# Gate/up biases added in PSUM by TensorE, down weights loaded in 8 KB runs: a 32-expert MoE block on one core

## What is computed

```python
def expert_block(args):
    xblk, e = args
    gu = xblk @ w_gu[e] + b_gu[e]
    x_glu = jnp.minimum(gu[:, :F], SWIGLU_LIMIT)
    x_lin = jnp.clip(gu[:, F:], -SWIGLU_LIMIT, SWIGLU_LIMIT)
    act = x_glu * jax.nn.sigmoid(SWIGLU_ALPHA * x_glu) * (x_lin + 1.0)
    return act @ w_down[e] + b_down[e]
```

## Time and profile before

| what | value |
|---|---|
| median of 3 runs (lowest, highest) | 1308.76 us (1308.35, 1309.82) |
| the profiled execution: its own time, its span | 1308.46 us, 1306.7 us |
| TensorE matmuls busy | 1103.0 us (84%) |
| VectorE busy | 1141.0 us (87%) |
| ScalarE busy | 950.8 us (73%) |
| GpSimd busy | 180.7 us (14%) |
| moved by the DMA queues | 445.55 MB, 341 GB/s over the span |
| packets under 8 KB, of all | 54273 of 87354 |

### The profile page before, as it was taken

How to read it: one execution, slowest core, us unless ns; L and a number is a source line. 1 busy time by engine, 2 the same in 40 slices (tenths; PEclk the granted TensorE clock), 3 DMA queues, 4 the chain that set the end, 5 groups by cost and what they waited for, 6 DMA issues and landing times.

```text
span 1306.7 us, 48498 instructions
## 1 busy us (share of the span) xinstructions
PE 1103.0 (84%) x21802; PEld 967.7 (74%) x21803; DVE 1141.0 (87%) x868; ACT 950.8 (73%) x881; POOL 180.7 (14%) x69
## 2 busy tenths in 40 slices
PE   5999998788888888888888888888888888888874
PEld 2455555788888888888888787887878888878873
DVE  5742544799999999999999999999999999999994
ACT  5232423578888888888888888888888888888873
POOL 0121200003333333200000020000200000100020
PEclk9999998899999999999999999999999999999987
DMA  9512221899999999999999999999999999999964
GB/s 348 209 43 87 95 115 65 316 361 379 404 405 405 405 405 406 405 405 402 398 401 399 398 397 403 402 397 394 403 403 398 399 402 396 402 401 396 397 251 142
DMA packets 87354, 445.55 MB, mean 341 GB/s; under 512 B 8897, under 2 KB 9409, under 8 KB 54273
## 3 DMA queue, kind: packets, MB, share of 16 engines
q1 hardware_dynamic: 82400, 427.99, 81.3%
q0 software_dynamic: 3472, 12.19, 4.8%
q10 hardware_dynamic: 1296, 2.44, 0.6%
HBM read 426.21 MB, written 16.38 MB: 339 GB/s over the span
## 4 chain that ended last, share of the span: by engine, by line
DVE 30%; DMA 28%; PE 18%; issue 17%; ACT 5%; DVEq 0%; SPq 0%; ACTq 0%
DVE ring L393 21%; DMA ring<-in_w_down_dram 14%; DMA ring<-in_w_gu_dram 9%; PE ps L1079 8%; PE ps L1181 4%; DMA arena<-in_w_gu_dram 4%; ACT ring L390 4%; PE ps L413 3%; DVE arena L468 2%; DVE arena L480 1%; DVE arena L483 1%; DVE arena L474 1%; DMA arena<-in_x_dram 1%; DVE arena L489 1%; PE ps L1117 1%
## 5 line engine op out<-in xcount | busy, mean ns | idle before, releaser
L413 PE MATMUL ps<-arena,ring 128*128 128x88 f16 x18432 | 783.2, 206 | 156.4 <-DVE ring L393 99.0
L413 PEld LDWEIGHTS ps<-arena,ring 128*128 128x128 f16 x18432 | 743.5, 100 | 188.2 <-DVE ring L393 96.4
L393 DVE SCALAR_TENSOR_TENSOR ring<-ring 128x2048 f16<-128x2048 f32 x290 | 655.3, 2285 | 23.2 <-ACT ring L390 22.0
L390 ACT ACTIVATE ring<-ring 128x2048 f16<-128x2048 f32 x290 | 549.9, 1907 | 111.8 <-DMA ring<-in_w_gu_dram 62.6
L463 POOL DMA_INDIRECT acc<-arena,slot_row x31 | 155.7, 5021 | 969.6 <-ACT arena L500 969.6
L393 DVE SCALAR_TENSOR_TENSOR ring<-arena,ring 128x2048 f16<-128x2048 f32 x94 | 212.9, 2285 | 5.6 <-ACT ring L390 4.8
L390 ACT ACTIVATE ring<-arena 128x2048 f16<-128x2048 f32 x94 | 178.9, 1907 | 27.2 <-DMA arena<-in_w_gu_dram 21.3
L406 PE MATMUL ps<-arena 128*128 128x88 f16 x2048 | 93.6, 207 | 6.6 <-DVE count_max_i L1594 3.3
L406 PEld LDWEIGHTS ps<-arena 128*128 128x128 f16 x2048 | 86.3, 101 | 7.6 <-issue 7.5
L1079 PE MATMUL ps<-ring,arena 128*128 128x512 f16 x384 | 87.5, 387 | 0.9 <-DVEq L1406 0.9
L1079 PEld LDWEIGHTS ps<-ring,arena 128*128 128x128 f16 x384 | 38.0, 99 | 45.2 <-issue 2.8
(11 more groups left out here) (136 smaller groups left out, 540.9 us busy)
## 6 DMA issues: line engine op xcount, KB each, us to landing
ring<-in_w_gu_dram SPq DMA_DIRECT2D x194, 1024.0 KB, 17.2
ring<-in_w_down_dram SPq DMA_DIRECT2D x96, 1024.0 KB, 15.5
arena<-in_w_gu_dram SPq DMA_DIRECT2D x62, 1024.0 KB
arena<-in_w_down_dram SPq DMA_DIRECT2D x32, 1024.0 KB
ring<-in_w_in_dram SPq DMA_DIRECT2D x4, 2048.0 KB, 12.6
ring<-in_w_out_dram SPq DMA_DIRECT2D x2, 2048.0 KB, 8.7
arena<-in_x_dram SPq DMA_DIRECT2D x4, 512.0 KB, 11.9
ring<-in_w_in_dram SPq DMA_DIRECT2D x2, 1024.0 KB, 11.2
```

Of the source, the lines that this page charges most:

```text
L390: return act.activation(split_of(slot)[:, 0, :], raw(r), ACT.Copy, scale=SCALE_W)
L393: return dve.scalar_tensor_tensor(split_of(slot)[:, 1, :], raw(r), SCALE_W, split_of(slot)[:, 0, :], ALU.mult, ALU.subtract)
L413: mm = pe.matmul(o, w[:, i, col:col + P], src[:, j, k, :], start=start and n == 0, stop=stop and n == 2, skip_group_check=True)
```

## The change

1. **Down weights.** `load_dn` gives partition p the rows 2p and 2p+1 of the chunk's 256, which lie side by side in HBM, as one run of 8 KB; before, it took rows p and 128+p, as two runs of 4 KB.
2. **Order of the hidden features.** The down product contracts over the features that stand on the partitions. So the gate/up product must now put feature 2p on partition p of one tile and 2p+1 in the next. It does so by its stationary operand: every second column of 256 (`every_other`, `gu_cols`), where it took 128 adjacent ones. The down product's stationary operand stays contiguous.
3. **Bias.** `pe_bias` starts the sums of an expert in `GU`: 16 matmuls whose stationary operand is the bias rows (float16 high and low parts of the 32 experts on 64 partitions, in the tile `late`) and whose moving operand is one column of `own`, repeated 88 times, that picks the expert. The gate/up products add to that.
4. **Clamps.** `dve_bias` is gone. `dve_glu` and `dve_lin` read `GU` in PSUM; the second signals `gu_taken`. The scale is folded into the limits and into the two instructions that follow.
5. **Front part.** The load of b_gu (256 KB) moves from the start of ScalarE's queue to SyncE's, behind the retention transposes, and happens twice (for the high and the low rows). The transposes and copies of the biases go. ScalarE makes the high part of the biases between the second and third tile of the router's work, VectorE the low part before the last residual add. `small` is 16 KB larger.

```diff
         def load_dn(sp, j, e, slot):
-            src = w_down[0, bass.ds(e, 1), 2 * j * P:2 * (j + 1) * P, :].rearrange("a (j p) c -> p (a j) c", p=P)
-            return sp.dma_start(raw(slot).rearrange("p (j c) -> p j c", j=2), src)
+            src = w_down[0, bass.ds(e, 1), 2 * j * P:2 * (j + 1) * P, :].rearrange("a (p i) c -> (a p) (i c)", i=2)
+            return sp.dma_start(raw(slot), src)
...
-        def gu_tile(b, j):
-            return 2 * b + j if j < 2 else NF // 2 + 2 * b + j - 2
+        def every_other(first):
+            return slice(first, first + 2 * P - 1, 2)
+
+        def gu_cols(b, j):
+            return every_other(F * (j // 2) + 2 * b * P + j % 2)
+
+        def pe_bias(pe, e):
+            for b in range(GB):
+                for j in range(PER):
+                    pe.matmul(GU[:, b, j * CAP:(j + 1) * CAP], bgu_parts[:, gu_cols(b, j)],
+                              own[:, bass.ds(e, 1)].to_broadcast([P, CAP]), start=(j == 0), stop=False,
+                              skip_group_check=True)
...
-        def dve_bias(dve, e):
-            return dve.scalar_tensor_tensor(
-                gub.rearrange("p b h (j c) -> p b (h j) c", j=2), GU.rearrange("p b (j c) -> p b j c", j=PER), UNSCALE,
-                bguT[:, bass.ds(e, 1), :].rearrange("p a (b j) -> p (a b) j", b=GB).unsqueeze(3)
-                .to_broadcast([P, GB, PER, CAP]), ALU.mult, ALU.add)
+        LIM = LIMIT / UNSCALE
 
         def dve_glu(dve):
-            return dve.tensor_scalar(gub[:, :, 0], gub[:, :, 0], LIMIT, None, ALU.min)
+            return dve.tensor_scalar(gub[:, :, 0], GU[:, :, 0:2 * CAP], LIM, UNSCALE, ALU.min, ALU.mult)
 
         def dve_lin(dve):
-            return dve.tensor_scalar(gub[:, :, 1], gub[:, :, 1], LIMIT, -LIMIT, ALU.min, ALU.max)
+            return dve.tensor_scalar(gub[:, :, 1], GU[:, :, 2 * CAP:4 * CAP], LIM, -LIM, ALU.min, ALU.max)
...
             early(0)
             early(1)
+            sp.wait_ge(mix_turned, H)
+            for i in range(2):
+                sp.dma_start(bgu_raw[32 * i:32 * i + E, :], b_gu[0]).then_inc(bgu_loaded, 16)
...
             def stage(s, q, last=False, more_meta=True):
+                pe.wait_ge(gu_taken, s)
+                pe_bias(pe, s)
                 pe.wait_ge(xT_ready, 2 * s + 2)
-                pe.wait_ge(gu_taken, s)
                 for k in range(4):
                     gate_up(s, q, k, k)
...
             for t in range(NT):
+                if t == NT - 1:
+                    dve.memset(late[64:P, :], 0.0)
+                    dve.wait_ge(bgu_high, 1)
+                    dve.scalar_tensor_tensor(bgu_parts[32:64, :], bgu_raw[32:64, :], SCALE_W, bgu_parts[32:64, :],
+                                             ALU.mult, ALU.subtract).then_inc(bgu_ready, 1)
                 residual(t)
```

More of the change, by code:

```diff
@@ L155, in build_program @@
         ranks = sm[:, 384:384 + RANKS]
+        own_f = sm[:, 384 + RANKS:384 + RANKS + E]
         tri = sb("tri", [P, P], BF16)
         ones = sb("ones", [P, P], BF16)
[L158 removed]
+        late = sb("late", [P, 2 * W])
+        rw_sb = late[:, 0:W]
+        wp_sb = late[:, W:2 * W].rearrange("p (h c) -> p h c", h=H)
+        bgu_parts = late.bitcast(F16)
+        own = sb("own", [P, E], F16)
         wr_sb = sb("wr_sb", [P, KD, E])
         br_sb = sb("br_sb", [P, E])
[L161 to L162 removed]
         ps_w = sb("ps_w", [P, H])
@@ L201, in build_program @@
         turned = [("x", t, i) for t in range(NT) for i in range(2)]
-        turned += [("qk", n) for n in range(2)] + [("bgu", j) for j in range(4)] + [("qk", n) for n in range(2, 8)]
+        turned += [("qk", n) for n in range(2)] + [("qk", n) for n in range(2, 8)]
         turned += [("s", h, i) for h in range(H) for i in range(NT)]
@@ L318, in build_program @@
         scattered = sem("scattered")
-        more = {k: sem(f"more_{k}") for k in ("high", "low", "used", "onehot", "gathered", "xT", "biased",
+        more = {k: sem(f"more_{k}") for k in ("high", "low", "used", "onehot", "gathered", "xT",
                                               "glu", "lin", "prod", "sig", "act32", "ah", "act", "yT", "turned",
@@ L408, in pe_gather, with product @@
             return mm
-        def product(pe, o, w, col, src, k, start, stop):
+        def product(pe, o, w, cols, src, k, start, stop):
             for n, (i, j) in enumerate(((0, 0), (0, 1), (1, 0))):
-                mm = pe.matmul(o, w[:, i, col:col + P], src[:, j, k, :], start=start and n == 0,
+                mm = pe.matmul(o, w[:, i, cols], src[:, j, k, :], start=start and n == 0,
                                stop=stop and n == 2, skip_group_check=True)
@@ L1046, in _ @@
             pe.wait_ge(small_loaded, 16)
-            def turn_bgu():
-                pe.wait_ge(bgu_loaded, 16)
-                for j in range(4):
-                    take(pe, ("bgu", j))
-                    pe.transpose(bank(("bgu", j))[:, 0:P], bgu_raw[:, j * P:(j + 1) * P], ident).then_inc(bgu_turned, 1)
             def turn_x(t):
@@ L1395, in _ @@
             dve.tensor_copy(tri[:, :], tri_f).then_inc(consts_made, 1)
+            dve.tensor_copy(own[:, :], own_f)
             def low_h(t):
@@ L1430, in _ @@
             low_win(1, 0)
-            def turned_bgu():
-                for j in range(4):
-                    dve.wait_ge(bgu_turned, j + 1)
-                    dst = bguT[:, :, :].rearrange("p e (ql b qh r) -> p e qh ql b r", ql=2, b=2, qh=2)[
-                        :, :, :, :, j // 2, j % 2]
-                    ins = dve.tensor_copy(dst, bank(("bgu", j))[:, 0:P].rearrange(
-                        "p (e qh ql) -> p e qh ql", e=E, qh=2))
-                    free(ins, ("bgu", j))
             def rotate(n):
@@ L1618, in gates_and_meta, with taken @@
                 dve.sem_inc(routed, 1)
-            def biased(e, done, first=False):
+            def taken(e, done, first=False):
                 dve.wait_ge(chunk_used, done)
```

64 lines of the change are left out of this document (29 added, 35 removed).

## The result

| | median us | lowest, highest | runs |
|---|---|---|---|
| before | 1308.85 | 1308.35, 1309.82 | 4 |
| after | 1301.57 | 1300.88, 1302.31 | 4 |

The ratio is 0.9948 (95% interval 0.9933 to 0.9962): the change makes the kernel 7.3 us faster. The forecast was 1296 us, 12.1 us faster, in a range of 1283 to 1307. The profiled execution of after took 1302.11 us with a span of 1300.2.

The account below looks back on a forecast made before the run. The prediction took weight supply to bound the late stages, with VectorE close behind. Down loads -9.5, tail -1.2 and start -1.0 and -0.4 summed to -12.1 us: 1308.5 to 1296 us, range 1283 to 1307.

Parts of the forecast that it names:

- The runs: Down-weight loads in 8 KB pieces: 0.19 us saved in each of 6 early stages, 0.38 in 22 late, -9.5 us.
- Bound by the supply of weights: Late expert stages: weight loading sets their 32.66 us, with VectorE, 2% idle, close behind.
- The clamp from PSUM: VectorE's two clamps per stage: 0.80 us each from PSUM instead of 0.44, VectorE's stage falling from 31.66 to 30.85 us.
- The tail: After 1225 us, VectorE's bias instruction gone and clamps changed: -1.2 us (0 to -1.7).
- The start: Front part: bias transposes gone from TensorE, -1.0 us, and 256 KB no longer sharing queues with x, -0.4 us.
- TensorE: Expert stages: 16 bias matmuls, 0.64 us a stage, hidden in 3.74 us of idle time, so 0.
- Strided stationary operands: Gate/up matmuls: weight loads with a step of two elements stay hidden under the matmul, so 0.
- rival 1: Gate/up matmuls: step-of-two weight loads not hidden, TensorE 37.3 us a stage, some 1440 us; chance 0.10.
- Rival 2: Down loads: piece size doesn't matter, only start and tail gain, 1306 us, late stages still 32.6 us; chance 0.16.
- Rival 3: Weight queues: mixing 4 and 8 KB packets was the loss and goes, 0.83 us a stage, 1283 us; chance 0.12.
- Theory B: Posed after the result: 8 KB pieces give 0.38 us a late stage, but TensorE's added work gives part back.
- Theory C: Posed after the result: the whole 7.3 us gain comes from the 8 KB down loads.

Follow-up runs that it names:

- run 8: The changed kernel with one more clamp from PSUM in every stage, written where nobody reads it: 1302.37 us.
- run 5: The changed kernel with GpSimd's scatter of each stage replaced by a 512-byte transfer: 1275.47 us.
- 6: The kernel before with GpSimd's scatter of each stage replaced by a 512-byte transfer: 1287.05 us.
- run 1: The kernel before with only the 8 KB down runs and the every-second-column gate/up operands, bias still on VectorE: 1302.23 us.
- run 4: The changed kernel with the 16 bias matmuls of each expert issued twice, the bias still counting once: 1314.51 us.
- run 10: No reference computation: 1408 matmuls of 128x88 on TensorE four times, with idle queues, gate/up, 4 KB down and 8 KB down streams; each group of 128 takes 5.19 us.
- run 9: No computation, only weight chunks streamed: down in 4 KB runs 410 GB/s, down in 8 KB 422, gate/up 422, mixed 417 with 4 KB and 422 with 8 KB.
- runs 1 to 3: Run 1, run 2, and as third the changed kernel with only the down loads back in 4 KB runs: 1308.37 us.
- run 2: The kernel before with only the bias matmuls, clamps from PSUM and new front part, down weights in 4 KB runs: 1308.06 us.

## Why the prediction was right, and which terms were mis-sized

- **The runs** (forecast -9.5): right in mechanism, 6.6 measured, 0.24 us a stage with bounds of 0.17 to 0.30. The early term's 0.19 lies within them; the late 0.38 was mis-sized: it came from taking a 415 GB/s window apart, against 423. Its 407 GB/s for 4 KB runs is 410 by themselves, its 423 is 422, and with these it is 0.29. This term is most of the 4.8 us by which the forecast was too high. The windows of the earlier trace rows were short (8 to 19 us) and differ by more than the size of the runs, as their own spread of 399 to 415 shows.
- **Bound by the supply of weights**: right. The scatter, to which the forecast gave no price, is a part of that supply: 2.0 us of a stage of 32.5. Run 8 puts all of VectorE's saving back, and the time doesn't follow; without the scatter (5, 6) VectorE takes over, with 30.86 and 31.67 us a stage where its sums had said 30.85 and 31.66.
- **The clamp from PSUM**: 0.88 us long, 0.80 from start to start, as taken. The Trainium skill's rule on PSUM operands ("VectorE: DVE Perf Modes", Why PSUM operands drop a tier) agrees with that row. The stages in which VectorE binds became 30.86 us, where 30.85 was worked out. The two clamps in after:

```profile
285.23 0.88 DVE L482 TENSOR_SCALAR arena<-ps 128x704 f32<-128x704 f32 x1
286.03 0.88 DVE L485 TENSOR_SCALAR arena<-ps 128x704 f32<-128x704 f32 x1
```

- **The tail** (forecast -1.2): half of it. ScalarE's last high parts of down chunks start at the same times in after and in run 1, although VectorE has the bias more to do there: most of VectorE's saving ends in a wait for a chunk. From the last chunk on 0.64 us of it is left. After, then run 1 (ScalarE's high parts of two down chunks, then the chain):

```profile
1247.53 1.91 ACT L393 ACTIVATE ring<-ring 128x2048 f16<-128x2048 f32 x1 [0.58 <-DMA ring<-in_w_down_dram]
1256.65 1.91 ACT L393 ACTIVATE ring<-arena 128x2048 f16<-128x2048 f32 x1 [0.50 <-DMA arena<-in_w_down_dram]
...
1261.48 0.81 DVE arena L497
...
1262.38 5.51 PE ps L416 x96
```

```profile
1247.46 1.91 ACT L390 ACTIVATE ring<-ring 128x2048 f16<-128x2048 f32 x1 [0.48 <-DMA ring<-in_w_down_dram]
1256.66 1.91 ACT L390 ACTIVATE ring<-arena 128x2048 f16<-128x2048 f32 x1 [0.49 <-DMA arena<-in_w_down_dram]
...
1262.12 0.81 DVE arena L491
...
1263.02 6.28 PE ps L413 x96
```

  The chain that ended last named VectorE there, but a chunk's landing stood 1 us behind. The next 96 matmuls take 0.77 us less in after; nothing in the change shortens them, and these are two executions only.
- **The start** (forecast -1.4 in two terms): the chain's first gather came 1.17 us sooner, but the rows above show the last chunks landing at the same times as in run 1, which has no such start. So in these executions it was used up by the supply before the end. The bias part alone gained 0.8 us, tail included; its interval (0 to 2.4 us) doesn't tell that from zero.
- **TensorE** (forecast: 0.64 a stage hidden in 3.74 free): the result was right, the size of the cover wrong, so that this term came out at 0 in part by luck. Run 4 shows 12.9 of the next 20.5 us. Idle time with the releaser "issue" is no cover, and it is not a fixed 1.42 a stage: it is a stop that hides behind a wait for VectorE, and comes out when that wait goes (65.3 to 24.9 us, while "issue" goes from 26.1 to 49.2). It is not VectorE's freed time that does this: run 8 has VectorE as busy as before, and yet 52.6 us of "issue" and only 21.8 of waits for VectorE. Why those waits shrink is open. A stage of after has 668 matmuls (64 gather, 4 meta, 16 bias, 576 products, 8 turns); at 6.20 us for 128 they would need 32.4 us of 32.53. That is the upper end: run 5 shows stages of 30.86, in which the instructions come faster, every 5.93 us.
- **Strided stationary operands** (rival 1, 1440 us): without a price. 128 gate/up products in a row, all with every second column, take 5.19 us in after; 128 matmuls with adjacent columns take the same 5.19 in run 10, 0.0405 each, and before it was 9.57 / 240 = 0.040. The forecast had taken this 0 from the nearest row and not shown it. Run 1, which has these loads, is faster by the runs' whole worth.
- **Rival 2** (size doesn't matter) falls by run 9 and runs 1 to 3. Its sign, late stages of 32.6 us, nearly came (32.53), but the sign was a poor one: shorter early stages leave longer late ones (run 2). **Rival 3** (mixing was the loss) too: with 8 KB in both, mixing costs nothing, and with 4 KB runs the mixture's 417 GB/s lies midway between 410 and 422, so it never cost anything. What set apart the two windows was something else.

The row on the 128 products, in the chain of after:

```profile
516.08 5.19 PE ps L416 x128
```

Theory B is half right: TensorE is close to being the bound and is it with 16 more matmuls. But run 1, with no bias on TensorE, has the same 0.24 us a stage, so the bias on TensorE gave back nothing that shows. Theory C holds: 6.6 of 7.3.

Open is where the 0.05 us a stage between the stream alone (0.29) and the kernel (0.24, bounds 0.17 to 0.30) goes, if it goes anywhere, why instructions came more slowly in one stretch of run 5, and why TensorE waits less for VectorE in after.

## What to carry to other kernels

Where queues that never run dry set the end, count all that they carry: here 4 KB runs cost 3% of their bytes' time, and eight filler rows of a scatter cost some 2.6 to 3.9 us, a third to a half of what that whole edit gained. Time saved on an engine that is merely second is worth nothing until the first bound is moved, so try it again then (0.8 us here, if anything, and a share of 11.6 once the scatter was gone). Price a size or a rate with a stream that does nothing else before taking windows of a busy kernel apart, and don't count idle time of TensorE as free before something was put into it.

## What the hardware showed that was not expected

- TensorE stops for 1.0 us after every 128 matmuls of 128x88 when the DMA queues are loaded, and never when they are idle (run 10): 16% of its rate, 6.20 us for what takes 5.19. The page lists a queue of kind "instruction" with packets of 16 KB (run 10: 44 packets, 0.72 MB), which is 64 bytes for each of 256 instructions; 44 x 256 = 11264 are just the 5632 matmuls and their weight loads. The trace has the start and end of each packet, and they tie the stop to the wait for one of them. All 28 stops of run 10 end 1.2 to 1.6 us after the end of such a packet. With idle queues a packet starts 0.0 to 0.4 us after TensorE enters its next 128 matmuls; beside streams mostly 3.5 to 3.8 us after. Its own time does not grow: 1.0 to 1.1 us beside streams, 0.9 to 1.4 without. So what grows is the time until it starts, and 3.6 + 1.1 + 1.5 us make the 6.2; what sets the 3.6 is not shown.
- The same stop is in the full kernel. Gaps of more than 0.6 us between TensorE's weight loads, from 600 to 1200 us, that end 1.1 to 1.7 us after an instruction packet: 37 of 96 in before, 65 of 88 in after, and all 86 in run 4.

The instruction queue's row on the page of run 10:

```profile
q8 instruction: 44, 0.72, 0.8%
```

- The Trainium skill ("Runtime: NRT & Kernel Launch", Instruction fetch mechanics) says that instructions come in blocks of 16 KiB, 256 in each, and that this fetch is hidden, as dispatch is slower than the fill. The block agrees with the trace (packets of 16 KB, and in run 10 a stop every 256 instructions). That it is hidden holds here with idle queues alone.
- A scattered row of 4 KB takes the queues as long as 8 KB of weights: 4.8% x 16 x 1300.2 us over 31 x 96 rows is 0.34 us a row, where an 8 KB packet at 422 GB/s over 16 engines is 0.31.
